# Encoder trunk on one core: the router's logits taken from the residual sums, with the norm's mean and deviation applied to the logits

## What is computed

```
x    = layer_norm(ALPHA * x + mix, ln1_g, ln1_b)         # x1, 768 x 1024
scores = sigmoid(x @ w_router)                           # 16 experts
biased = scores + b_router
# best group of 4 by its two best experts, then the two best experts inside it
w_sel  = scores of those two, divided by their sum
for e in range(16):
    y += gates[:, e] * ((silu(x @ w_gate[e]) * (x @ w_up[e])) @ w_down[e])
out  = layer_norm(ALPHA * x + y, ln2_g, ln2_b)
```

## Time and profile before

| what | value |
|---|---|
| median of three executions | 777.86 us (777.48 to 779.97) |
| profiled execution | 779.4 us, of which the span of the profile is 777.6 us |
| PE / DVE / ACT / POOL busy | 732.2 / 579.5 / 482.9 / 252.6 us |
| TensorE's granted clock, mean | 0.987 of full speed |
| bytes moved | 179.37 MB, 231 GB/s in the mean |

### The profile page before, as it was taken

How to read it: one execution, slowest core, us unless ns; L and a number is a source line. 1 busy time by engine, 2 the same in 40 slices (tenths; PEclk the granted TensorE clock), 3 DMA queues, 4 the chain that set the end, 5 groups by cost and what they waited for, 6 DMA issues and landing times. The chain is left out here.

```text
span 777.6 us, 12791 instructions
## 1 busy us (share of the span) xinstructions
PE 732.2 (94%) x3881; PEld 603.2 (78%) x3881; DVE 579.5 (75%) x975; ACT 482.9 (62%) x881; POOL 252.6 (32%) x294
## 2 busy tenths in 40 slices
PE   3999999999999899999998899999999999999984
PEld 3898888888888677768786678888888888878862
DVE  6964365556555776685798888888888888889847
ACT  3334355556655665675147368788788888888825
POOL 3132257656664252344411101221222221222111
PEclk9999999999999999999999899999999999999998
DMA  9723311222034853311756759999999999999763
GB/s 342 258 109 129 109 59 44 83 68 68 2 122 143 300 232 121 123 68 45 289 200 270 271 190 383 382 374 381 386 372 372 385 375 374 393 379 389 258 217 162
DMA packets 71485, 179.37 MB, mean 231 GB/s; under 512 B 11687, under 2 KB 28071, under 8 KB 71444
## 3 DMA queue, kind: packets, MB, share of 16 engines
q1 hardware_dynamic: 66692, 166.34, 56.6%
q0 software_dynamic: 4752, 12.51, 6.5%
HBM read 153.20 MB, written 30.42 MB: 236 GB/s over the span
## 5 line engine op out<-in xcount | busy, mean ns | idle before, releaser
L1290 POOL TENSOR_SCALAR me<-me,mrec 128x512 f32<-128x512 f32 (+1 forms) x48 | 65.7, 1370 | 52.2 <-DVE mrec L1469 52.1
L1952 DVE TENSOR_TENSOR eDl<-rawD,eDh 128x1024 fp32r<-128x1024 f32 x68 | 81.2, 1217 | 0.2
L1952 DVE TENSOR_TENSOR eUl<-rawU,eUh 128x1024 fp32r<-128x1024 f32 x68 | 78.8, 1220 | 0.3 <-ACT eUh L1882 0.3
L1952 DVE TENSOR_TENSOR eGl<-rawG,eGh 128x1024 fp32r<-128x1024 f32 x64 | 74.1, 1217 | 1.4 <-ACT eGh L1882 1.4
L2073 POOL DMA_INDIRECT acc_rows<-yg,idx_s x16 | 25.6, 1602 | 134.5 <-ACT yg L1907 134.5
L1882 ACT ACTIVATE eDh<-rawD 128x1024 fp32r<-128x1024 f32 x64 | 64.8, 1053 | 2.4 <-DMA rawD<-in_w_down 2.3
L1882 ACT ACTIVATE eGh<-rawG 128x1024 fp32r<-128x1024 f32 x64 | 62.8, 1052 | 2.1 <-DMA rawG<-in_w_gate 1.9
L1882 ACT ACTIVATE eUh<-rawU 128x1024 fp32r<-128x1024 f32 x64 | 62.3, 1050 | 0.0
L1797 PE MATMUL bank<-eGh,xgT_h 128*128 128x512 f32 x136 | 55.9, 411 | 1.8 <-issue 1.0
L1797 PE MATMUL bank<-eUh,xgT_h 128*128 128x512 f32 x136 | 54.6, 401 | 0.0
L1799 PE MATMUL bank<-eGl,xgT_h 128*128 128x512 f32 x136 | 54.2, 398 | 0.0
(11 more groups left out here) (353 smaller groups left out, 2156.1 us busy)
## 6 DMA issues: line engine op xcount, KB each, us to landing
rawG<-in_w_gate SPq DMA_DIRECT2D x68, 512.0 KB, 9.7
rawU<-in_w_up SPq DMA_DIRECT2D x68, 512.0 KB, 9.5
rawD<-in_w_down SPq DMA_DIRECT2D x68, 512.0 KB, 10.9
wb_raw<-in_w_in SPq DMA_DIRECT2D x8, 512.0 KB, 4.7
wo_raw<-in_w_o SPq DMA_DIRECT2D x8, 512.0 KB, 7.8
xln_rows<-res SPq DMA_DIRECT2D x6, 512.0 KB, 3.8
dqk_high<-st_h SPq DMA_DIRECT2D x8, 384.0 KB, 2.3
dqk_low<-st_l SPq DMA_DIRECT2D x8, 384.0 KB, 3.3
```

The lines of the kernel that those rows point to most:

```text
L1290: nc.gpsimd.tensor_scalar(e, e, mrec[:, g % NSB:g % NSB + 1], None, ALU.mult).then_inc(m_p, 1)
L1952: nc.vector.tensor_tensor(wl_[X][i][:], raw_of(X, t, i)[:], f32(wh_[X][i][:]), ALU.subtract).then_inc(s_lo[X], 1)
```

## The change

The logits no longer wait for the norm. PE turns the sums y = `res` as soon as DVE has added a half (`turn_y(t, hf)`), with every fourth column of a half taken for one transpose; the partial sums use the router's weights times the norm's scale, and an extra column of 1/1024 that gives the mean. The fold matrix gets the term that subtracts the mean, DVE multiplies each tile's logits by 1/deviation and subtracts the offset (`minus_logits`), and ACT's exponential is one operation on the result. x1 goes to new buffers (`cen`) for tiles 0 to 3, since `res` is still being turned. POOL prepares the weights (`router_weights`, six small operations ahead of tile 1's power), one product sums them (`weight_sums`), and DVE makes the fold matrix in tile 2 (`folding`). SP loads the router's weights in two pieces and two small columns of scale and offset.

Beside it: `g0_low(2)` and `g0_low(3)` move from behind tile 5 to behind `idx_tab`; all of `low_part("U", 0)` and the gate values (L2535) move behind `x_low(0, 1)`; the gate-slot products move behind `inner("U", 0)`; the unread products become 23, 23, 20 and a new 3 instead of 16, 18 and 16; the load of the third tile's gate weights waits for the first gather.

The core of the diff:

```diff
@@ tensor
+            def turn_y(t, hf):
+                pe.wait_ge(s_y, 12 + 2 * t + hf + 1)
...
+                wait(pe, s_x1e, 2 * (t - 2) + hf + 1)
...
+                half = res[:, t, hf * HW:(hf + 1) * HW].rearrange("p (m j) -> p j m", j=4)
+                for j in range(4):
+                    last = nc.tensor.transpose(bank[:, j * P:(j + 1) * P], half[:, j, :], ident[:])
...
+                if t == 1:
+                    pe.wait_ge(s_rt, 80 + 8)
+                if t >= 2:
+                    pe.wait_ge(s_rexp, t - 1)
...
-            for k in range(16, 18):
-                front_o_part(k, 0, 12)
-            turn_x1(0)
-            for t in range(3, NT):
-                front_o_part(12 + 2 * t, 0, 12)
+            turn_y(0, 0)
+            turn_y(0, 1)
+            front_o_part(16, 0, 12)
+            turn_y(1, 0)
+            turn_y(1, 1)
+            weight_sums()
+            front_o_part(17, 0, 12)
+            part_sums(0)
+            turn_y(2, 0)
+            front_o_part(18, 0, 12)
+            turn_y(2, 1)
+            part_sums(1)
+            logits(0)
+            for t in range(3, NT - 1):
                 front_o_part(13 + 2 * t, 0, 12)
-                part_sums(t - 3)
-                if t > 3:
-                    logits(t - 4)
-                turn_x1(t - 2)
-            turn_x1(4)
-            part_sums(3)
-            logits(2)
+                turn_y(t, 0)
+                part_sums(t - 1)
+                logits(t - 2)
+                front_o_part(14 + 2 * t, 0, 12)
+                turn_y(t, 1)
+            front_o_part(23, 0, 12)
+            turn_y(5, 0)
             part_sums(4)
             logits(3)
-            turn_x1(5)
+            turn_y(5, 1)
+            logits(4)
             part_sums(5)
-            logits(4)
             logits(5)
...
-            keep_busy(16)
+            keep_busy(23)
...
-            keep_busy(18)
+            keep_busy(23)
...
-            keep_busy(16)
-            pe.wait_ge(s_vals, 2)
-            for n in range(2 * NT):
-                last = nc.tensor.matmul(psum[7][:, 0:3 * MAX_TILES], hot[:, n, :],
...
-            experts_pe(pe)
+            keep_busy(20)
+            experts_pe(pe, keep_busy)
@@ experts_pe
         turn_x(0)
+        keep_busy(3)
         inner("G", 0, range(4))
         turn_x(1)
         inner("U", 0, range(4))
+        pe.wait_ge(s_vals, 2)
+        for n in range(2 * NT):
+            last = nc.tensor.matmul(psum[7][:, 0:3 * MAX_TILES], hot[:, n, :], gate_vals[:, n].rearrange("p a b -> p (a b)"),
@@ vector
+                    if hf == 0 and t >= 3:
+                        minus_logits(t - 3)
...
-                then(nc.vector.scalar_tensor_tensor(out=res[:, t, :], in0=res[:, t, :], scalar=mv[:, t, 0:1], in1=ln1g_sb[:],
...
+                if t == 2:
+                    folding()
+                if t == NT - 1:
+                    minus_logits(t - 2)
+                then(y_centred(t))
+                if t == NT - 1:
+                    minus_logits(t - 1)
+                    minus_logits(t)
+                x1_shifted(t)
...
-            for i in range(2, 4):
-                g0_low(i)
...
+            dve.wait_ge(s_rexp, NT + 1)
...
             tt(idx_tab[:], idx_f[:], psum[5][:, MAX_TILES:2 * MAX_TILES], ALU.add).then_inc(s_idxtab, 1)
-
+            for i in range(2, 4):
+                g0_low(i)
@@ experts_dve
-        low_part("U", 0, (0,))
         x_low(0, 0)
         x_low(0, 1)
-        low_part("U", 0, (1, 2, 3))
+        low_part("U", 0)
+        gate_values()
         low_part("D", 0)
         low_part("G", 1)
@@ sync
-            sp.dma_start(wr_sb[:, :, 0:NE], w_router.rearrange("(c p) n -> p c n", p=P)).then_inc(s_rt, 16)
+            for h in range(2):
+                sp.dma_start(wr_sb[:, 4 * h:4 * h + 4, 0:NE],
...
+            for i, v in enumerate((ln1_g, ln1_b)):
+                sp.dma_start(gb_col[:, i, :].rearrange("p (h j) -> p h j", h=2),
...
+            sp.wait_ge(s_gather, 16)
             for i in range(4):
                 sp.wait_ge(s_raw["G"][i], 32)
                 sp.dma_start(unit_dst("G", i, 2), unit_src("G", 2, i)).then_inc(s_raw["G"][i], 16)
```

More of the change, by code:

```diff
@@ L382, in encoder_trunk @@
     W_BANKS = (7, 4)
+    cen = [at(f"cen{i}", (42, 50, 54, 58)[i], [P, D]) for i in range(4)]
     ln1g_sb = at("ln1g_sb", 30, [P, D])
@@ L1869, in experts_pe @@
         inner("U", 0, range(4))
+        pe.wait_ge(s_vals, 2)
+        for n in range(2 * NT):
+            last = nc.tensor.matmul(psum[7][:, 0:3 * MAX_TILES], hot[:, n, :], gate_vals[:, n].rearrange("p a b -> p (a b)"),
+                                    start=(n == 0), stop=(n == 2 * NT - 1))
+        last.then_inc(s_gslots, 1)
         count = iterate(pe, iteration)
@@ L2269, in x1_scaled @@
                     act.wait_ge(s_stored[t % 2], 16 * (t // 2))
-                nc.scalar.activation(ax[t % 2][:], res[:, t, :], ACT.Copy, scale=ALPHA).then_inc(s_ax, 1)
+                nc.scalar.activation(ax[t % 2][:], x1_tile(t), ACT.Copy, scale=ALPHA).then_inc(s_ax, 1)
             def part_copied(t):
@@ L2368, in g0_low, with y_centred, x1_shifted, folding @@
                 nc.vector.tensor_tensor(wl_["G"][i][:], raw["G"][i][:], f32(wh_["G"][i][:]), ALU.subtract).then_inc(s_lo["G"], 1)
+            def y_centred(t):
+                if t >= 4:
+                    dve.wait_ge(s_x1t, 2 * (t - 4) + 2)
+                return nc.vector.scalar_tensor_tensor(out=x1_tile(t), in0=res[:, t, :], scalar=mv[:, t, 0:1], in1=ln1g_sb[:],
+                                                      op0=ALU.subtract, op1=ALU.mult)
+            def x1_shifted(t):
+                dve.wait_ge(s_rstd, NT + t + 1)
+                nc.vector.scalar_tensor_tensor(out=x1_tile(t), in0=x1_tile(t), scalar=rstd[:, t:t + 1], in1=ln1b_sb[:],
+                                               op0=ALU.mult, op1=ALU.add).then_inc(s_x1, 1)
+            def folding():
+                dve.wait_ge(s_log, 1)
+                nc.vector.scalar_tensor_tensor(out=fold_all[:], in0=psum[3][:, 0:NE], scalar=fold[:, NE:NE + 1], in1=fold[:, 0:NE],
+                                               op0=ALU.mult, op1=ALU.subtract).then_inc(s_rt, 1)
+                nc.vector.tensor_copy(wr_off[:], psum[3][:, NE:2 * NE]).then_inc(s_rt, 1)
+            def minus_logits(t):
+                dve.wait_ge(s_log, logits_done(t))
+                dve.wait_ge(s_rstd, NT + t + 1)
+                dve.wait_ge(s_rt, 80 + 8)
+                nc.vector.scalar_tensor_tensor(out=sg[:, t, :], in0=psum[2 + t % 2][:, P + t * NE:P + (t + 1) * NE],
+                                               scalar=rstd[:, t:t + 1], in1=wr_off[:], op0=ALU.mult,
+                                               op1=ALU.subtract).then_inc(s_rexp, 1)
             for t in range(NT):
@@ L2533, in _, with gate_values @@
             then(nc.vector.tensor_copy(gate_part[:, 2, :], gate_rest[:, 1, :]))
-            for j in range(3):
-                last = tt(gate_vals[:, :, j, :], in_tile[:], gate_part[:, j, :].unsqueeze(2).to_broadcast(full), ALU.mult)
-            last.then_inc(s_vals, 1)
-            experts_dve(dve)
+            def gate_values():
+                for j in range(3):
+                    last = tt(gate_vals[:, :, j, :], in_tile[:], gate_part[:, j, :].unsqueeze(2).to_broadcast(full), ALU.mult)
+                last.then_inc(s_vals, 1)
+            experts_dve(dve, gate_values)
 def tables():
```

151 lines of the change are left out of this document (90 added, 61 removed).

## The result

The change made the kernel slower. The median went from 778.35 us (777.48 to 779.97, four runs) to 784.61 us (783.81 to 784.80, four runs): ratio 1.0084, 95% interval 1.0069 to 1.0100, 6.3 us more. The forecast was 780.4 with a range up to 782.8. The profiled execution took 784.8 us, its span is 782.9 us; before it was 779.4 and 777.6.

A forecast was written before the change was run, and what follows sets the result against it. PE was taken to bound the expert loop, DVE the norm stage and the date of tile 1's first products. Terms -0.5 + 0 + 1.0 + 2.0 = +2.5 us on the median 777.86 gave 780.4, range 776.6 to 782.8.

The forecast's parts named there:

- Norm stage: Up to the sigmoid: last add 3.0 us later, way behind it 3.8 shorter, 0.3 for stride; -0.5 us in all.
- rival C: Norm stage: strided loads are dear, each of eleven half turns about 0.2 us more; 782.4 us, chance 0.12.
- Routing and what lies behind it: Sigmoid to table unchanged at 12.5 us; g0_low (2.35) and gate operations fit in 7.03 us before x_low(0, 0): 0.
- The sentence on the moved loads: First gather: an x_low(0, 0) that moves against the sigmoid would mean the gather feels the moved loads; no size given.
- slack until the third pass: Third tile's load, moved behind the gather, is not needed before the loop's third pass; no cost counted.
- DVE's list: From x_low(0, 0) to x_low(1, 0): a low part and gate values added, ACT wait gone; 16.7 us, +1.0.
- The clock: Ahead of tile 1: PE idles some 4 us, clock falls, dense stretch opens slower; +2.0 us, bounds 1.7 to 2.5.
- ends in a wait: First expert's products at full clock gain 2.5 us, but PE then waits for tile 1, so the gain is lost.
- one that lands sooner: First gather: landing sooner was given 0.01 within the chance of a faster result.
- B: Ahead of the second tile: no clock fall, so -0.5 + 1.0 = +0.5; 778.4 us, chance 0.28.
- D: Norm stage: PE keeps pace, DVE stays the bound, last add before 406.5; -2.5, 775.4 us, chance 0.12.
- The signs of error named at the end: Last add before 406.5, G0 again 8 us without gap, turns well above 1.1 us, or x_low(0, 0) moving against the sigmoid.

The follow-up runs named there:

- loads held: The change, with SP's loads of units 2 and 3 of the second tile's gate weights held until the first gather landed: 782.35 us, ratio 1.0045.
- low parts later: The change, with g0_low of units 2 and 3 behind the gate's small operations instead of ahead of them: 780.70 us, ratio 1.0023.
- the sums behind: The change with both loads held, DVE's list restored, and tile 4's partial sums and fold product behind both turns of tile 5: 777.76 us, ratio 0.9993.
- more loads: The change, with all four second-tile gate loads held until the table stands, the third tile's no longer held for the gather: 784.90 us, ratio 1.0084.
- fillers in the kernel before: The kernel before with only the change's unread products (23, 23, 20 and three behind the first turn): 779.10 us, ratio 1.0009.
- the list put back: The change, with gate values and first up low part again ahead of x_low(0, 0), gate-slot products ahead of the first expert's: 780.92 us, 1.0026; again 781.77, 1.0024.
- the kernel before with the moved low parts: The kernel before with g0_low of units 2 and 3 behind the table and third-tile gate loads behind the first gather: 780.92 us, ratio 1.0022.

## Why the prediction was wrong

**Norm stage: forecast -0.5, measured 0.0.** Right in its mechanism. PE became the bound: no gap on PE in tiles 3 to 5, and DVE waits 2.21 us for a part in tile 3. Against the add of part 10 the last add came 3.5 later (forecast 3.0), and the sigmoid 5.40 behind it (forecast 5.1). The half microsecond missing ahead of the last add is in the turns: a half turn with partial sums behind it takes 0.56 from start to start, with products behind it 0.38, and I had counted 0.41 for all:

```profile
398.87 0.63 PE L2191 MATMUL bank<-ident,res 128*128 128x128 f32 x4
399.25 0.48 PE L673 MATMUL bank<-wo_h,mixD_h 128*128 128x512 f32 x1
...
402.10 0.63 PE L2191 MATMUL bank<-ident,res 128*128 128x128 f32 x4
402.66 0.65 PE L2212 MATMUL bank<-x1T,wr_sb 128*32 128x128 f32 x16
```

The stride, of which rival C was made, cost PE nothing that shows, and the 0.3 us that I took for it were not needed. Its loads take 208 ns in the mean of the norm stage, exactly those of `xg`, and 0.38 is not more than half a turn of before. Nor is the 0.56 the stride's: in the kernel before, with adjacent columns, the last turn ahead of partial sums was longer, too, two turns taking 1.87 us where one with products behind it takes 0.82:

```profile
406.05 1.94 PE L2167 MATMUL bank<-ident,res 128*128 128x128 f32 x16
407.92 0.64 PE L2180 MATMUL bank<-x1T,wr_sb 128*32 128x128 f32 x16
```

The loads of the change:

```profile
L2191 PEld LDWEIGHTS bank<-ident,res 128*128 128x128 f32 x48 | 7.3, 208 | 0.8 <-issue 0.2
```

So the rule on cache lines (the Trainium skill, "Advanced Engine Details and Errata", "SBUF Cachelines") is not what these loads follow: one hit on a line costs as much as two, and both cost more than four.

**Routing and what lies behind it: forecast 0, measured 4.1.** This is the step that failed. It said that `g0_low` "fit below the 7.03 us until `x_low(0, 0)`", and checked that for DVE alone. I did not ask who waits for `g0_low`: SP, with two loads of 512 KB, which so were moved into the flight of the gather, the one transfer in this stretch that nothing covers. The sentence on the moved loads spoke of the third tile's, which were held for the gather, and had no word on the second tile's. It also asked of the third tile's only when they are needed ("slack until the third pass"), not what they meet: they meet the second gather, which took 7.4 us instead of 4.3, and PE waited 0.64 us for it. Without the two loads in its flight the first gather is back at 4.5 us and `x_low(0, 0)` at 7.16 behind the table (loads held); moving their issue by 2.4 us does the same (low parts later). The price could be bounded from the profile of before: there the first two gathers land in 4.3 and 4.4 us, and those of the loop, beside a full stream of loads, in 8.6:

```profile
DMA to landing us min/median/max: 4.3/8.6/8.8
```

That is up to 4.3 us, and no row of it stood in the prediction.

**DVE's list: forecast +1.0, measured +1.05.** Right, by its working: 438.77 to 455.57 are 16.80 us (forecast 16.7). Putting it back together with the held loads recovered all: 4.2 us between the ratios 1.0045 and 0.9991. That is more than this term; with the same list the run of the sums behind shows 34.8 us from the sigmoid to tile 1 against 37.0 with held loads alone, and the clock that does not fall there gives 1.4 more; the rest, about 0.6, is not accounted for.

**The clock: forecast +2.0, measured 0 ahead of tile 1 in this kernel.** The mechanism exists, but the place moved. With the late gather PE waited 5.04 us ahead of the first turn, the clock fell there (0.62 at 435), and the turn and the first five products ran at the lower level; what that cost DVE is within the 4.11 of the gather. PE so ended the first expert's products 1.0 us later than in the run with more loads (446.43 against 445.43), then waited for the second gather, and only 1.93 us of the forecast 4 remained ahead of tile 1, where the clock held:

```profile
455.00:456.00 1.00, 0.00 (x0) 0.00 (x0) 0.93 (x5) 0.00 (x0) 0.00 (x0) 1.00 0.58 238
456.00:457.00 1.00, 0.65 (x3) 0.59 (x4) 0.84 (x2) 0.00 (x0) 0.18 (x1) 1.00 0.02 8
```

In three other kernels the fall came ahead of tile 1: with held loads, with fillers in the kernel before, and with more loads on the gather, where the wait was the forecast 4 us. The first half of tile 1 then took 1.4, 1.25 and 1.56 us longer, less than the 1.7 to 2.5 that I had as bounds. How much of it reaches the end is not told apart: from the first product of tile 1 to the end of the span these three take 327.1 to 327.9 us and the other eleven 325.3 to 327.1. With the low parts later, and in two of the kernels with held loads, the fall came behind the wait for the second gather instead. That gain of the first products "ends in a wait", as forecast, was confirmed by the fillers alone; that the wait can be filled, and the gain kept, I had not worked out.

**The rivals.** None had a late gather (one that lands sooner had a chance of 0.01), and so none gave the time. What B asked for came about: no fall ahead of the second tile. But the cause was the late gather, which B did not have either, and its 778.4 is further off than the forecast. C did not occur: half turns took at most 0.16 more than the 0.41 counted, and not because of the stride. D did not: the last add came at 409.75, far from 406.5. The signs of error named at the end held the right one, a `x_low(0, 0)` that moves against the sigmoid, without a price or a chance. With 0.0 + 4.1 + 1.05 + 0 the sum is 5.2, against 5.3 in the spans and 6.3 in the medians; the profiled execution of the kernel before lay 1.05 us above its median.

## What to carry to other kernels

An operation that is moved into a free stretch of its engine takes along all that is released by it: follow its semaphore to the queues, and ask what their transfers meet at the new date. A transfer that nothing covers, like a gather on which a stage opens, is best alone in flight while its rows move; loads that are not urgent can be held until it has landed, and one has then to see which transfer they meet next (here the third tile's loads met the second gather). A gain ahead of a wait is worth nothing by itself, and may go back when the longer wait drops the clock; a few unread products in that wait kept the gain here.

## What was not expected of the hardware

- The first gather asks for 128 rows but moves 81 rows of 4 KB in this input, 0.33 MB; with the two loads 1.38 MB were moved until 436.9, at 94 to 299 GB/s, where other stretches move over 370. It is not the sum of bytes that made the gather late: in the run with more loads 295 to 422 GB/s were moved from 431 to 437, and it landed in 8.0, no later than with two units. Loads that were issued up to 2.1 us ahead of it, as in the kernel before, did it no harm: its rows moved there from 430.4 to 432.5, and only 0.03 MB of loads with them. By the Trainium skill, "DMA: Bandwidth & Descriptors", "Queues, rings and completion order", each DMA engine takes turns between the queues that have work, a packet at a time. The traces agree: in the second profile of the list put back, packets of loads and rows of the gather alternate from 434.5 to 436.4, 0.16 us each, and nothing else moves. The busy share (ahead of the last column) is then 0.06, one engine of sixteen:

```profile
434.00:435.00 1.00, 0.00 (x0) 0.00 (x0) 0.69 (x1) 0.00 (x0) 0.00 (x0) 1.00 0.08 29
435.00:436.00 1.00, 0.00 (x0) 0.00 (x0) 0.00 (x0) 0.00 (x0) 0.00 (x0) 1.00 0.06 25
```

  But for seven, the rows were through by 433.2; in this profile the gather landed with its slowest engine. An equal share of all engines would make its 0.33 MB only about 0.9 us longer at the 371 GB/s of the earlier trace rows (an estimate), and 3.1 to 4.1 were seen. Why one engine falls so far behind, and why two profiles of six escaped with 4.8 and 5.6, stays open.
- The clock's answer to a wait of PE of about 2 us differs: it fell behind waits of 1.77, 1.79, 1.91, 1.94, 2.03 and 2.08 us, in six profiles, and held behind 1.76, 1.79 (twice), 1.85, 1.93 and 2.18 us, in five. The 1.79 us of the earlier trace rows, from which the prediction took that such a wait drops the clock, came again at the same place of the kernel before with the moved low parts, and there the clock held.
